# Two transformer blocks with product-key experts: six more early expert inputs, a later last sum of the gather, joint norms at the block border, and retention heads in pairs

## The chip, the cores and the metric

One core of a Trainium2 chip runs the kernel, one launch for the whole computation. The metric is the device time of one execution in microseconds (us), lower is better. PE is TensorE (PEld its weight loads), DVE is VectorE, ACT is ScalarE, POOL is GpSimd, SP is SyncE, which here issues the weight stream's DMAs.

## What is computed

256 tokens of width 1024 pass two blocks, each of depth one, all in float32. The first block modulates and normalises x, runs a bidirectional retention over 8 heads (64 key columns, 128 value columns), a Fourier mix, gates both, and adds a convolutional feed-forward of width 2816; it ends with a norm. The second block normalises again, runs an RWKV-7 and an mLSTM branch, merges them, and adds PEER: product-key retrieval among 128 x 128 single-neuron experts. Cut to what the change touches:

```python
# retention, per head; state s comes from the context tokens
intra_decay = where(diff >= 0, exp(lg * maximum(diff, 0)), 0)
o_f = (q @ k.T * intra_decay) @ v + (q * exp(lg * (pos + 1))) @ s
o = o_f + flip(o_b)                       # diagonal counts twice
# end of block 1, start of block 2
x = rms_norm(x, final_norm_w)
h = _rmsnorm(x, norm1_g)                  # norm of a norm
# PEER
s = einsum('nhpc,hpkc->nhpk', q, sub_keys)
s_top, i_top = top_k(s, 16)               # for both halves
best, pos = top_k(s_top[0][:, None] + s_top[1][None, :], 16)
expert = i_top[0] * 128 + i_top[1]        # at pos
gate = softmax(best)
act = gelu(u_emb[expert] . tok) * gate
out = sum(act * v_emb[expert])
```

## The kernel before

All activations lie transposed, features on the partitions and 256 tokens along the row. Weights come as one stream of pages of 1 MB (two blocks of 128 x 1024), which SP loads into a ring of three. Two ways of multiplying are used. In the split way ACT writes a rounded copy of a block (`split`, L1031, the "hi" part), DVE subtracts it for the rest (L1442, the "lo" part), and PE sums three fp32r products of each tile; three pairs of such pieces lie in SBUF, and `piece_used` frees them. In the `whole` way PE multiplies the fp32 block straight from the ring (L434 is the helper line of every matmul); the profile shows two MATMUL instructions for each such product.

Every engine's order is written out by hand, and semaphores carry the data flow. What the steps of the prediction touch:

**Retention** (`scores`, `outputs` on PE; `decay_exp` L1163 on ACT; `decay_arg` L1591 and the product L1612 on DVE; L360 on POOL). Head after head: DVE computes the exponent (L1593, L1594), ACT its Exp (L1165), POOL multiplies by a mask that doubles the diagonal (L360), DVE multiplies the scores by it (L1612), PE forms the output, ACT copies it (L1172). There are two buffers of each kind. Even heads use partitions 0 to 63 of the array's rows, odd heads 64 to 127. The Fourier products follow (L434 on `fT`).

**Block border** (`x_norm`). The last residual of block one, its squares on ACT (L1078), their sum by a matmul with ones, Ln and Exp on ACT (L1084, L1085), eight scalings on DVE into x (L1500); then squares, sum, Ln, Exp and eight scalings once more for block two's input h, and its hi and lo parts.

**Search** (`select`, `gather` L1991 on DVE, `number` L405 and L411 on POOL). For each of 8 heads DVE finds the 16 best keys of both halves for 256 tokens, forms the pair sums (L2017, L2019), finds the 16 best pairs, and marks their places (L1983). POOL turns the marks into key numbers: two multiplications (L405) and three halvings (L411). DVE does the last halving (L1991), for the head before, ahead of its own pair sums. Meanwhile PE makes queries and key scores, then the inputs of seven early experts (`early_up`), whose gelus ACT writes into `early`.

**Scatter.** After the transposes of the choice (L948) and an eighth early input, the gates of every token are laid out as a 128 x 128 matrix, first key by second key: a product of two one-hot matrices per token. DVE writes the column one-hots (L2086) and half of the row one-hots (L2083), ACT the other half (L1383 Square, L1390 Relu), PE multiplies, and ACT copies four tokens at a time into G (L1372). It is a loop of 16 tokens a pass; PSUM banks 6, 7, 0 and 1 take turns.

**Experts.** Expert e's input product (`up`, 24 fp32r matmuls of 256 columns) gives its activation, ACT its gelu (L1405), DVE multiplies by the gates and splits the result (`gate`, L2102, L2105, L2107), and `down` (12 matmuls of 512 columns) adds its output to four PSUM banks. First come six `down` alone, for experts whose inputs were made early; then a loop of 120 pairs of `down(e - 2)` and `up(e)`; then two `down`. The first page's split lies before the scatter: on ACT amid the early gelus, on DVE just ahead of the one-hots.

The modulation weights of the feed-forward come by 16 loads that POOL issues (L347), each after a step of DVE, two under way at most; their descriptors use a scratch area at the bottom of SBUF, above which `early` lies.

## Time and profile before

| what | us |
|---|---|
| median of 3 runs (lowest, highest) | 1901.5 (1900.65, 1904.35) |
| the profiled execution, its time | 1900.2 |
| its span, first to last instruction | 1898.4 |
| PE busy, share of the span | 1744.8, 92% |
| DVE busy | 1192.0, 63% |
| ACT busy | 826.4, 44% |
| POOL busy | 117.7, 6% |
| mean granted TensorE clock, as a share of full speed | 0.955 |

The profiled time is the span and 1.8 us around it. Busy shares are averages over stages with quite different limits, so they say little about one stage. A row of the timeline gives the start and the length of a run of like instructions, then engine, line, operation, tiles and count, and in brackets the engine's idle time before it with what ended it. Matmuls overlap, so their busy times add up to more than their spacing: start-to-start times are what counts. A granted clock of 1.00 is 2.4 GHz and 0.50 is 1.2 GHz; values between are mixtures over a stretch.

### The profile page before, as it was taken

What the parts mean: (1) busy time and instruction counts of PE and PEld (TensorE: products, weight loads), DVE (VectorE), ACT (ScalarE), POOL (GpSimd) and SP (SyncE); (2) the same over time, 40 slices, a digit from 0 to 9 for tenths busy, and PEclk for the clock granted to TensorE, in tenths of its full rate; (3) what the DMA queues carried; (4) which work ended last, traced back from release to release, by engine and by line L of the source; (5) the groups of instructions that cost most, each with busy time, mean ns of one, the idle gap of its engine ahead of it and who ended that gap; (6) DMA issues with size and microseconds to landing.
All of it is one profiled execution on the core that took longest, in us unless ns stands there. A gap on an engine that the chain in (4) does not pass through costs nothing.

```text
span 1898.4 us, 31715 instructions
## 1 busy us (share of the span) xinstructions
PE 1744.8 (92%) x11856; PEld 1584.1 (83%) x11856; DVE 1192.0 (63%) x2141; ACT 826.4 (44%) x1236; POOL 117.7 (6%) x130
## 2 busy tenths in 40 slices
PE   8799899899999979698899677999999999999997
PEld 1799868899998967596788566799999999999997
DVE  0647456577644658741448899666666666666665
ACT  2334435466544466221331299344444444444443
POOL 0000010022100000140003300000000000000000
PEclk9899899899999979796799899999999999999999
DMA  8566304455553522100234210455555555555553
GB/s 319 210 261 244 112 25 154 168 179 183 178 178 117 190 93 67 45 1 1 89 111 134 89 45 0 146 186 184 192 180 195 179 193 181 189 187 184 192 180 119
DMA packets 38521, 279.03 MB, mean 147 GB/s; under 512 B 4401, under 2 KB 4529, under 8 KB 5041
## 3 DMA queue, kind: packets, MB, share of 16 engines
q1 hardware_dynamic: 35136, 254.82, 39.3%
q0 software_dynamic: 2304, 16.78, 2.3%
q10 hardware_dynamic: 1008, 6.41, 0.9%
q8 instruction: 53, 0.87, 0.2%
q14 instruction: 20, 0.16, 0.0%
HBM read 276.94 MB, written 1.05 MB: 146 GB/s over the span
## 4 chain that ended last, share of the span: by engine, by line
PE 78%; DVE 10%; ACT 6%; POOL 2%; issue 2%; DMA 1%; ACTq 0%; SPq 0%; POOLq 0%; DVEq 0%
PE ps L434 78%; DVE piece L1442 1%; DMA ring<-in_stream 1%; ACT small L1383 1%; POOL arena L405 1%; POOL arena L411 1%; ACT piece L1031 1%; DVE arena L1752 1%; DVE arena L1983 1%; ACT small L1390 1%; DVE arena L1921 0%; DVE arena L1500 0%; DVE arena L1525 0%; DVE arena L1844 0%; ACT arena L1138 0%
## 5 line engine op out<-in xcount | busy, mean ns | idle before, releaser
L434 PEld LDWEIGHTS ps<-h_r,piece 128*128 128x128 f32 x5808 | 727.5, 195 | 38.0 <-issue 25.4
L434 PE MATMUL ps<-h_r,piece 128*128 128x256 f32 x5808 | 735.3, 287 | 22.1 <-DVE h_r L1506 9.5
L1442 DVE TENSOR_TENSOR piece<-ring,piece 128x1024 fp32r<-128x1024 f32 x440 | 541.9, 1238 | 309.3 <-ACT piece L1031 309.3
L1031 ACT ACTIVATE piece<-ring 128x1024 fp32r<-128x1024 f32 x440 | 461.6, 1056 | 401.9 <-PE ps L434 387.1
L434 PE MATMUL ps<-piece,late_r 128*128 128x512 f32 x1536 | 373.6, 393 | 6.0 <-DVE late_r L2107 6.0
L434 PEld LDWEIGHTS ps<-piece,late_r 128*128 128x128 f32 x1536 | 281.6, 189 | 60.9 <-issue 5.7
L2102 DVE TENSOR_TENSOR late<-late,arena 128x256 f32<-128x256 f32 x120 | 76.5, 637 | 125.9 <-ACT late L1405 125.9
L434 PE MATMUL ps<-arena 128*64 128x128 f32 (+8 forms) x696 | 124.3, 373 | 29.5 <-DVE hx L1855 9.0
L434 PEld LDWEIGHTS ps<-arena 128*128 128x128 f32 (+4 forms) x696 | 93.8, 203 | 57.0 <-issue 14.7
L1405 ACT ACTIVATE late<-ps 128x256 f32<-128x256 f32 x120 | 46.2, 385 | 213.4 <-PE ps L434 213.4
L434 PE MATMUL ps<-arena,ring 128*128 128x256 f32 x384 | 85.9, 384 | 1.6 <-DVE arena L1500 1.6
L434 PEld LDWEIGHTS ps<-arena,ring 128*128 128x128 f32 x384 | 73.4, 193 | 11.9 <-issue 2.0
L1053 ACT ACTIVATE arena<-ps 128x512 f32<-128x512 f32 x43 | 25.7, 597 | 107.0 <-PE ps L434 107.0
L434 PE MATMUL ps<-ffn_hi,piece 128*128 128x256 f32 x352 | 63.5, 283 | 0.8 <-DVE piece L1442 0.8
L2107 DVE TENSOR_TENSOR late_r<-late,late_r 128x256 fp32r<-128x256 f32 x128 | 54.4, 425 | 4.4
L434 PE MATMUL ps<-hx,arena 128*128 128x128 f32 (+1 forms) x352 | 50.9, 285 | 6.4 <-DVE hx L1855 5.6
L434 PEld LDWEIGHTS ps<-ffn_hi,piece 128*128 128x128 f32 x352 | 54.9, 192 | 1.0 <-DVE piece L1442 1.0
L434 PE MATMUL ps<-mg_hi,piece 128*128 128x256 f32 x256 | 49.2, 294 | 6.0 <-DVE mg_lo L1468 6.0
L434 PE MATMUL ps<-arena,pconst_sb 128*128 128x256 f32 (+1 forms) x136 | 48.7, 505 | 4.4 <-ACT arena L1078 2.6
L434 PEld LDWEIGHTS ps<-hx,arena 128*128 128x128 f32 (+1 forms) x352 | 45.1, 196 | 6.9 <-DVE hx L1855 5.9
L434 PE MATMUL ps<-ffn_lo,piece 128*128 128x256 f32 x176 | 49.8, 283 | 0.0
L434 PEld LDWEIGHTS ps<-mg_hi,piece 128*128 128x128 f32 x256 | 42.3, 203 | 6.3 <-issue 6.3
(298 smaller groups left out, 1821.2 us busy)
## 6 DMA issues: line engine op xcount, KB each, us to landing
ring<-in_stream SPq DMA_DIRECT2D x240, 1024.0 KB, 5.0
arena<-in_mod POOLq DMA_DIRECT2D x16, 1024.0 KB, 5.9
arena<-in_const ACTq DMA_DIRECT2D x1, 2256.0 KB, 8.7
arena<-in_const ACTq DMA_DIRECT2D x1, 2000.0 KB, 9.3
xres<-in_xT SPq DMA_DIRECT2D x1, 1024.0 KB, 10.3
arena<-in_xT SPq DMA_DIRECT2D x1, 1024.0 KB, 12.3
arena<-in_subk ACTq DMA_DIRECT2D x1, 1024.0 KB, 4.9
out<-arena SPq DMA_DIRECT2D x2, 512.0 KB, 2.7
```

The lines of the kernel that those rows point to most:

```text
L405: g.tensor_tensor(e[:, 2 * c:2 * c + 2], e[:, 2 * c:2 * c + 2], topf[:, :, 2 * hh + c, :].unsqueeze(2).to_broadcast([P, 2, 16, 16]), ALU.m ...
L411: g.tensor_tensor(e[:, :, :, 0:m], e[:, :, :, 0:m], e[:, :, :, m:2 * m], ALU.add).then_inc(S["place_no"], 1)
L434: mm_last[0] = nc.tensor.matmul(*args, **kw)
L1031: A(piece[:, 0, c % 3], ring[:, p % RING, s], ACT.Copy).then_inc(S["hi_ready"], 1)
L1053: A(dst, ps[:, T % 2, src], func, **kw).then_inc(acc_free[T % 2], 1)
L1383: a = A(r[:, e, :], iota, ACT.Square, scale=-1.0, bias=selT[:, 0, bass.ds(16 * i + (4 * b + e), 1)])
L1390: A(r, r, ACT.Relu, scale=-1.0, bias=1.0).then_inc(S["row_hot"], 1)
L1405: A(gelu_t[:, e % 2, :], ps[:, T % 2, 0:L], ACT.Gelu).then_inc(acc_free[T % 2], 1)
L1442: TT(piece[:, 1, c % 3], ring[:, p % RING, s], piece[:, 0, c % 3].bitcast(F32), ALU.subtract).then_inc(S["lo_ready"], 1)
L1752: ins = STT(mqk[:, n, :], mqk_raw[:, n, tap:tap + L], cols[:, cq + 5 * n + tap:cq + 5 * n + tap + 1], mqk[:, n, :], ALU.mult, ALU.add)
L2102: TT(a_t, ready, G[:, :, bass.ds(LOOP * i + e, 1)].rearrange("p n a -> p (n a)"), ALU.mult).then_inc(S["a_chain"], 1)
L2107: TT(a_r[:, 1, b, :], a_t, a_r[:, 0, b, :].bitcast(F32), ALU.subtract).then_inc(S["a_ready"], 1)
```

## The change

- `EARLY` goes from 8 to 14. Of these, `CHOICE` = 10 are made where the eight were: nine before the transposes of the choice, the tenth after them. Four are made amid the scatter: each has 8 product steps, one behind each of 8 of 14 groups of four tokens, into bank 1, and its gelu is on ACT at group 13, 27, 41 and 55. The gates use three banks instead of four. PE's and ACT's part of the scatter is written out, 64 groups; DVE's stays a loop.
- The loop has 114 experts, and 12 `down` alone stand before it.
- The first page's hi part is copied by POOL, after its key numbers; DVE's lo part follows the one-hots.
- `gather(hh - 1)` moves behind the second search of `select(hh)`.
- At the border two sums are formed from the same squares, one with ones and one with weights `norm_w` = `final_norm_w`^2 + eps; h is scaled straight from x with `gain12` = `final_norm_w` x `norm1_g_2`. The block's own norm of x comes behind the first split of the next stage.
- In the retention POOL's mask is gone: ln 2 on the diagonal is added within the exponent. Scores and outputs are formed for two heads at a time, the 64-row matmuls of both heads in turn; there are four buffers of `probs`.
- `SCRATCH` goes from 4096 to 1024, and `h_full` moves to where G is written last.

```diff
-EARLY = 8
-SCRATCH = 4096
+EARLY = 14
+CHOICE = 10
+SCRATCH = 1024
...
-        h_full = w3(0, 8)
+        h_full = w3(30720, 8)
-        probs = w3(28160, 2, 512)
+        probs = w3(0, 4, 512)
-        gate_banks = (6, 7, 0, 1)
+        gate_banks = (6, 7, 0)
...
# POOL
-            pool.wait_ge(S["const1_in"], 16)
-            for hh in range(8):
-                pool.wait_ge(S["decay_exp"], hh + 1)
-                g.tensor_tensor(decay[:, hh % 2], decay[:, hh % 2], c1("mask12"), ALU.mult).then_inc(S["decay_m"], 1)
...
             for hh in range(7):
                 number(hh)
+            first = PAGE["first"]
+            for s in range(2):
+                c = piece_no(first) + s
+                if s == 0:
+                    pool.wait_ge(loaded[first % RING], 16 * (first // RING + 1))
+                pool.wait_ge(S["piece_used"], c - 1 - s)
+                g.tensor_copy(piece[:, 0, c % 3], ring[:, first % RING, s]).then_inc(S["hi_ready"], 1)
...
# PE, retention
+            def scores(m):
+                if m:
+                    pe.wait_ge(S["probs"], 2 * m)
+                for st in range(2):
+                    for e in range(2):
+                        r = 64 * e
+                        s_ = mm(ps[:, 4 + e, st * L:(st + 1) * L], qk[r:r + 64, 4 + m, st * P:(st + 1) * P],
+                                qk[r:r + 64, m, :], start=True, stop=True)
+                        if st == 1:
+                            s_.then_inc(S["scores"], 1)
+
+            def outputs(m):
+                pe.wait_ge(S["probs"], 2 * m + 2)
+                if m:
+                    pe.wait_ge(S["o_sb"], 2 * m)
+                for e in range(2):
+                    n = 2 * m + e
+                    for st in range(2):
+                        mm(ps[:, 6 + e, 0:L], v_tok[:, st, n * P:(n + 1) * P], probs[:, n % 4, st * L:(st + 1) * L],
+                           start=st == 0, stop=False)
+                for d, st_ in enumerate((st_f, st_b)):
+                    for e in range(2):
+                        r = 64 * e
+                        o = mm(ps[:, 6 + e, 0:L], st_[r:r + 64, m * P:(m + 1) * P], qdec[r:r + 64, 4 * d + m, :], start=False,
+                               stop=d == 1)
+                        if d == 1:
+                            o.then_inc(S["out_mm"], 1)
...
+            for m in range(4):
+                if m < 3:
+                    scores(m + 1)
+                outputs(m)
...
# PE, border
-            x_norm(1)
-
-            x_norm(2)
+            for k in range(8):
+                if k % 2 == 0:
+                    pe.wait_ge(S["xs_sq"], 4 + (k // 2 + 1))
+                mm(ps[:, 2, 0:L], ones, sq[:, k, :], start=k == 0, stop=k == 7)
+                m = mm(ps[:, 3, 0:L], norm_w[:, k, :], sq[:, k, :], start=k == 0, stop=k == 7)
+            m.then_inc(S["xs_mm"], 1)
...
# PE, scatter
+            def early_step(n):
+                e, k = CHOICE + n // 8, n % 8
+                T, p = TURN["peer"] + e, PAGE["early"] + e // 2
+                if k == 0:
+                    turn(T)
+                    turn(T + 1)
+                    pe.wait_ge(loaded[p % RING], 16 * (p // RING + 1))
+                m = mm(ps[:, 1, (T % 2) * L:(T % 2 + 1) * L], ring[:, p % RING, e % 2, k, :], h_full[:, k, :], start=k == 0,
+                       stop=k == 7)
+                if k == 7:
+                    m.then_inc(S["acc_ready"], 1)
...
+            for q in range(L // 4):
+                scatter(q)
+                n, k = (q - 3) // 14, (q - 3) % 14
+                if 0 <= n < EARLY - CHOICE and k < 8:
+                    early_step(8 * n + k)
...
# ACT
-            for n in range(8):
-                act.wait_ge(S["out_mm"], n + 1)
-                A(oT[:, n, :], ps[:, 6 + n % 2, 0:L], ACT.Copy).then_inc(S["o_sb"], 1)
-                if n < 6:
-                    decay_exp(n + 2)
+            for m in range(4):
+                if m < 3:
+                    decay_exp(2 * m + 2)
+                    decay_exp(2 * m + 3)
+                for n in range(2 * m, 2 * m + 2):
+                    act.wait_ge(S["out_mm"], n + 1)
+                    A(oT[:, n, :], ps[:, 6 + n % 2, 0:L], ACT.Copy).then_inc(S["o_sb"], 1)
...
-            x_norm(1)
-
-            for u in range(4):
-                x_squares(u)
-            x_norm(2)
+            act.wait_ge(S["xs_mm"], 2)
+            ac(A(rs, ps[:, 3, 0:L], ACT.Ln, scale=1.0 / D, bias=eps_sq))
+            A(rs, rs, ACT.Exp, scale=-0.5).then_inc(S["xs_root"], 1)
             for k in range(8):
                 act.wait_ge(S["hraw"], 24 + k + 1)
                 A(h[0][:, k, :], sq[:, k, :], ACT.Copy).then_inc(S["h_hi"], 1)
+            ac(A(rs_last, ps[:, 2, 0:L], ACT.Ln, scale=1.0 / D, bias=eps6))
+            A(rs_last, rs_last, ACT.Exp, scale=-0.5).then_inc(S["xs_root"], 1)
...
-            for e in range(5):
+            for e in range(CHOICE - 2):
                 early_gelu(e)
-            split(PAGE["first"])
...
+            for q in range(L // 4):
+                if q % 2 == 1:
+                    rows(q)
+                if q >= 2 and q % 4 != 1:
+                    gates_out(q - 2)
+                if q % 2 == 1:
+                    rows_end(q)
+                if q >= 2 and q % 4 == 1:
+                    gates_out(q - 2)
+                if late_e < EARLY and q == 13 + 14 * (late_e - CHOICE):
+                    T = TURN["peer"] + late_e
+                    act.wait_ge(S["acc_ready"], T + 1)
+                    A(early[:, late_e, :], ps[:, 1, (T % 2) * L:(T % 2 + 1) * L], ACT.Gelu).then_inc(acc_free[T % 2], 1)
+                    late_e += 1
...
# DVE
-                dv(TS(d, c1("dist_f"), lgrow[:, n:n + 1], None, ALU.mult))
+                dv(STT(d, c1("dist_f"), lgrow[:, n:n + 1], c1("ln2_same"), ALU.mult, ALU.add))
                 STT(d, c1("dist_b"), lgrow[:, 8 + n:9 + n], d, ALU.mult, ALU.add).then_inc(S["decay_arg"], 1)
...
+            TT(norm_w, ones.unsqueeze(1).to_broadcast([P, 8, P]), square1.unsqueeze(2).to_broadcast([P, 8, P]), ALU.mult)
             residual("dn", 40)
-            x_norm(1, xres, col("final_norm_w", 0, 8))
+            x_norm(1, sq, gain12)
+            stage("lora", 1)
+            dve.wait_ge(S["xs_root"], 3)
+            for k in range(8):
+                STT(xres[:, k, :], xres[:, k, :], last_w[:, k:k + 1], rs_last, ALU.mult, ALU.mult).then_inc(S["xfin"], 1)
...
                 second_places(srcs, vals, idxs, ready)
-                if hh:
-                    gather(hh - 1)
                 cd, u, v = cand[:, hh % 2], topv[:, :, 2 * hh, :], topv[:, :, 2 * hh + 1, :]
...
                 found[hh] = second_places(srcs, vals, idxs, ready)
+                if hh:
+                    gather(hh - 1)
...
-            split(PAGE["first"])
...
             with dve.Fori(1, L // 16) as i:
                 onehots(i)
+            split(PAGE["first"])
             dve.wait_ge(S["g_sb"], L // 4)
```

## Rows read from the trace of the kernel before

**Rows 1.** The page, part 4: chain of waits, shares of the span by engine.
```profile
PE 78%; DVE 10%; ACT 6%; POOL 2%; issue 2%; DMA 1%; ACTq 0%; SPq 0%; POOLq 0%; DVEq 0%
```
**Rows 2.** Busy time by stage: stretch, length, PE, PEld, DVE, ACT, POOL, clock, DMA.
```profile
1072.00:1093.00 21.00, 4.33 (x16) 3.51 (x15) 19.29 (x86) 3.43 (x7) 4.85 (x5) 0.62 0.15 50
1093.00:1184.40 91.40, 68.85 (x524) 61.90 (x522) 85.17 (x286) 87.01 (x225) 0.00 (x0) 0.99 0.06 23
1184.40:1208.40 24.00, 18.71 (x72) 14.41 (x72) 16.08 (x27) 6.37 (x6) 0.00 (x0) 0.93 0.28 91
1208.40:1883.00 674.60, 674.56 (x4321) 615.66 (x4322) 447.17 (x600) 289.00 (x359) 0.00 (x0) 1.00 0.54 183
```
**Rows 3.** Timeline of PE, second products alone, then the loop's first.
```profile
1194.51 5.72 PE L434 MATMUL ps<-piece,late_r 128*128 128x512 f32 x24 [1.30 <-DVE late_r L2107]
1201.53 5.70 PE L434 MATMUL ps<-piece,late_r 128*128 128x512 f32 x24 [1.30 <-DVE late_r L2107]
1208.44 3.02 PE L434 MATMUL ps<-piece,late_r 128*128 128x512 f32 x12 [1.21 <-DVE late_r L2107]
```
**Rows 4.** Timeline from the end of the search to the scatter's start.
```profile
1066.07 0.38 ACT L1053 ACTIVATE early<-ps 128x256 f32<-128x256 f32 x1 [3.07 <-PE ps L434]
...
1089.61 1.51 PE L948 MATMUL ps<-pconst_sb,arena 128*128 128x128 f32 x6 [16.67 <-DVE arena L2074]
...
1090.92 5.13 PE L434 MATMUL ps<-arena,ring 128*128 128x256 f32 x16
...
1097.44 0.69 DVE L2083 TENSOR_TENSOR row_more<-pconst_sb,late 128x512 f32<-128x512 f32 x1 [3.01 <-PE ps L434]
```
**Rows 5.** Timeline: two early gelus, a pass of the scatter, the first gate.
```profile
1085.04 0.66 ACT L1053 ACTIVATE early<-ps 128x256 f32<-128x256 f32 x2
...
1129.81 0.63 ACT L1390 ACTIVATE late<-late 128x512 f32<-128x512 f32 x1
...
1133.62 0.71 PE L434 MATMUL ps<-pconst_sb,small 128*128 128x128 f32 x4 [1.01 <-ACT small L1390]
...
1135.06 0.61 PE L434 MATMUL ps<-cols,late 128*128 128x128 f32 x4
...
1135.24 0.63 ACT L1390 ACTIVATE late<-late 128x512 f32<-128x512 f32 x1
...
1184.39 0.60 DVE L2102 TENSOR_TENSOR late<-early,arena 128x256 f32<-128x256 f32 x1 [2.59 <-ACT arena L1372]
```
**Rows 6.** Timeline of the retention: DVE and POOL, and the first Fourier weight loads.
```profile
240.68 0.75 DVE L1594 SCALAR_TENSOR_TENSOR arena<-arena,small 128x512 f32<-128x512 f32 x1
...
242.65 0.69 DVE L1612 TENSOR_TENSOR arena<-ps,arena 128x512 f32<-128x512 f32 x1 [1.23 <-POOL arena L360]
...
249.58 1.27 POOL L360 TENSOR_TENSOR arena<-arena 128x512 f32<-128x512 f32 x1 [1.63 <-ACT arena L1165]
249.66 1.74 DVE L1594 SCALAR_TENSOR_TENSOR arena<-arena,small 128x512 f32<-128x512 f32 x1
...
262.74 1.38 PEld L434 LDWEIGHTS ps<-arena 128*128 128x128 f32 x7 [0.33 <-issue]
```
**Rows 7.** The search: DVE's waits for POOL (total, times, longest), and one head's timeline.
```profile
DVE arena L1991 <- POOL arena L411: 9.2, 7, 1.3
...
1077.50 2.52 POOL L411 TENSOR_TENSOR arena<-arena 128x512 f32<-128x512 f32 x3
...
1080.24 0.28 DVE L2017 TENSOR_TENSOR arena<-arena 128x128 f32<-128x128 f32 x1
```
**Rows 8.** Busy time of a stretch of gram products, columns as in rows 2.
```profile
774.90:778.20 3.30, 3.29 (x28) 2.84 (x28) 2.12 (x4) 0.00 (x0) 0.00 (x0) 1.00 0.43 181
```
**Rows 9.** Timeline ahead of and at the block border.
```profile
503.36 2.36 DVE L1442 TENSOR_TENSOR piece<-ring,piece 128x1024 fp32r<-128x1024 f32 x2 [2.31 <-ACT piece L1031]
...
562.34 3.62 PE L434 MATMUL ps<-arena,pconst_sb 128*128 128x256 f32 x16
...
573.85 0.47 ACT L1084 ACTIVATE small<-ps,cols 128x256 f32<-128x256 f32 x1 [1.69 <-PE ps L434]
```

More of the change, by code:

```diff
@@ L939, in _, with early_up @@
             m.then_inc(S["x_in_psum"], 1)
-            for e in range(EARLY - 1):
+            def early_up(e):
+                T = TURN["peer"] + e
+                turn(T)
+                whole(PAGE["early"] + e // 2, e % 2, ps[:, T % 2, 0:L]).then_inc(S["acc_ready"], 1)
+            for e in range(CHOICE - 1):
                 early_up(e)
@@ L1359, in _ @@
                 A(selv[:, tt, 2, :], selv[:, tt, 2, :], ACT.Exp).then_inc(S["g_exp"], 1)
-            for e in range(5, EARLY - 1):
-                early_gelu(e)
+            early_gelu(CHOICE - 2)
             act.wait_ge(S["x_in_psum"], 1)
@@ L1394, in _, with rows @@
-            act.wait_ge(S["selt_sb"], 2)
-            rows(0)
-            with act.Fori(1, L // 16) as i:
-                rows(i)
-            gates_out(L // 16 - 1, 2)
-            gates_out(L // 16 - 1, 3)
+            def rows(q):
+                r = row_hot[q % 4]
+                if q >= 4:
+                    act.wait_ge(S["g_mm"], 2 * q - 6)
+                for e in range(4):
+                    a = A(r[:, e, :], iota, ACT.Square, scale=-1.0, bias=selT[:, 0, 4 * q + e:4 * q + e + 1])
+                a.then_inc(S["row_square"], 1)
```

137 lines of the change are left out of this document (50 added, 87 removed).

## The prediction

> **What bounds the kernel now.** I read the chain of waits by engine first: 78% of it is TensorE (PE), 10% VectorE (DVE), 6% ScalarE (ACT) [rows 1]. Then busy time by stage [rows 2]. From 1208.4 to 1883.0 us runs the expert loop, 120 experts in 674.6 us, 5.62 us each, with PE busy throughout: there time goes only if PE gets less work. Three stages ahead of it are bound otherwise. While the keys are searched (1072 to 1093) DVE is busy for 19.3 of 21 us and PE for 4.3. In the scatter (1093 to 1184.4) DVE (85.2 of 91.4 us) and ACT (87.0) are full and PE has room. From 1184.4 to 1208.4, second products alone, no engine is full. So this change is priced by the wait that ends last in each stage. What the measurement can tell from no change is 0.2%, 3.8 us.
>
> **The change, part by part.** I count against the profiled execution's own 1900.2 us (span 1898.4).
>
> *Six more early inputs.* Six experts leave the loop and join the stage of second products alone. In the loop each costs 5.62 us, 33.7 together. There, a pair of second products takes from 1194.51 to 1201.53 to 1208.44, 6.97 us on average, with PE idle for 1.2 to 1.3 us before each pair [rows 3]: the next page's second copy starts only when the pair's second product has taken its piece, and behind the copy come DVE's subtraction and gates. The code of this stage is unchanged, so three more pairs cost 20.9. Gain 33.7 - 20.9 = **12.8 us**; bounds 12 to 16.8 (PE work alone, 5.7 a pair).
>
> *Where the six products go.* One costs 8 steps of 0.43 us, 3.45 us from one gelu to the next [rows 4]. Two go into the search. Before, PE was idle for 16.67 us ahead of the transposes at 1089.61 [rows 4], and 6.9 us fit in it.
>
> *Four amid the scatter.* A full pass of 16 tokens lasts from 1129.81 to 1135.24, 5.43 us, and ACT has no idle in it [rows 5]. On PE two groups of four tokens take from 1133.62 to 1135.06 + 4 x 0.11, 1.9 us with the first fill, 0.89 a group. With a step in every group PE would need 4 x (0.89 + 0.43) = 5.3 us of the 5.43: it just fits, and only 8 of 14 groups carry a step. A step delays the next group by up to 0.43 us, and DVE and ACT have about 0.5 us before they need what PE frees. So the products cost nothing on the path. If that cover is gone, they cost 32 x 0.43 = 13.8 us, which is a rival. ACT is full, so its four gelus count: 0.33 us each [rows 5], with hand-over **+1.1 us** (0 to 1.5). Three gate banks in place of four change nothing: the copy asked for is always one behind ACT's last Relu.
>
> *First page's copies on POOL.* The page is loaded after the tenth early gelu, so POOL copies it in the scatter's first 15 us. The trace shows no such copy. What it shows is POOL and DVE side by side: a DVE operation of 0.75 us took 1.74 us when it began 0.08 us after a POOL operation of 1.27 us [rows 6], so DVE stood still for POOL. POOL's 512 elements with two inputs took 1.27; twice 1024 elements with one input cost between 2 x 1.27 and 4 x 1.27, less the 1.1 us by which DVE runs ahead of PE. Bounds 0 to +4.0; I take **+1.8**, near the lower end, as one input is read instead of two. The Trainium skill, "SBUF — State Buffer", section "Who interferes with whom", says that a DVE instruction with two SBUF inputs, or in a two-port mode, and a GpSimd instruction exclude each other for their whole length. By that rule alone both copies would be paid in full, +2.5 to +5. DVE's subtraction of this page moves behind the scatter, where DVE was idle for 2.59 us before its first gate [rows 5]; two operations of 1.2 us fit. Cost 0 (to +0.3).
>
> *The last early product.* It took 5.13 us for 16 matmuls at 1090.92, not 3.45: PE had been idle, and the granted clock was 0.62 in that stretch [rows 2, 4], so part of it ran at 1.2 GHz. DVE then waited 3.01 us for PE [rows 4]. With two more products PE now works until 1.3 us before the transposes. The product runs at 2.4 GHz: **-1.6 us** (-1.7 to 0). ACT now computes the gates' Exp after the eighth gelu and pays two table switches: **+0.4** (0 to 1.5).
>
> *Gather behind the second search.* DVE waited seven times for POOL's last sum, 9.2 us together [rows 7]. The sum is wanted 2.5 us later now, when POOL is done. But the two pair sums (L2017, L2019) that follow move up into POOL's three operations, which end at 1080.02 [rows 7], and they read two SBUF inputs as L1594 does. What is late next is the lock: between nothing gained and 9.2. POOL's work is three instructions, DVE waits only for the one under way, so I take 0.4 us lost a head: **-6.5 us**.
>
> *Retention in pairs.* Before, a head took about 2.9 us and DVE waited for POOL's mask at its start and end (1.23 us at 242.65) [rows 6]. Now POOL is gone, DVE has two operations of 0.75 and one of 0.69 us a head, 2.2 with hand-over, and PE interleaves the two row groups. That these overlap is seen in the gram products: 28 matmuls of alternating groups took 3.30 us [rows 8], when 20 of 256 columns at 0.216 (3.45 / 16 of the early product) and 8 of 128 at 0.11 would make 5.2 in sequence. So PE needs 0.9 + 1.7 + 0.9 + 0.2 = 3.7 us a pair and DVE 4.5: DVE is the bound. The first pair's probabilities are ready at 242.7 as before, then five decays and six products, 12.0 us, give 254.7. PE ends later: the third pair's outputs at 255.5, their copies at 256.3, the last outputs at 259.0. Before, the Fourier products began at 262.74 [rows 6]. **-3.7 us** (-5 to +2.5; the upper end if the groups don't overlap).
>
> *Joint norms.* Before: a sum from 562.34, 16 matmuls in 3.62 us, its root, eight scalings, squares, and a second sum whose root began at 573.85 [rows 9]. Now one stretch of 32 matmuls, 7.1 us, ends at 569.4 and the root follows: **-4.4 us** (-3.5 to -4.7). The scalings of x go behind a split and push the next one by 1.4 us, against 3.4 of lead. The added weights (about 1.9 us of DVE) fit into 2.31 us of idle at 501 [rows 9].
>
> *Smaller descriptor scratch.* It concerns POOL's 16 modulation loads alone, two of them under way at most; cost 0 (to +3).
>
> Sum: -12.8 + 1.1 + 1.8 - 1.6 + 0.4 - 6.5 - 3.7 - 4.4 = -25.7, so 1874.5 for the profiled execution. The median of the runs lies 1.3 us above it: **1875.8 us**.
>
> **Rivals.**
> A. *The scatter doesn't hide the steps.* PE in order, 5.3 of 5.43 us, every wait a little longer than counted: then the steps add up to 13.8 us. For it: the margin of 0.1 us. Against: steps in 8 of 14 groups only. 1889.6.
> B. *Row groups give nothing, or DVE stalls in the retention.* PE then needs 5.5 us a pair from 242.7, ending at 265: +2.5 in place of -3.7. For: head by head the same shapes ran one after the other at 0.216. Against: rows 8. 1882.
> C. *Slower: the scatter written out starves PE.* Sixteen passes of a loop become 64 groups in a line, so each instruction is fetched anew. To eat 25.7 us it must lengthen each group from 1.36 to 1.76 us; at 1.85 the 64 groups cost 31.4 and the time is 1875.8 + 31.4 = 1907. For: nothing in the loop shows fetching. Against: the gram stretch, itself in a line, ran 28 matmuls and 28 weight loads in 3.30 us [rows 8], 17 a us, where the scatter needs some 15.
>
> **How the numbers follow.** Forecast 0.74, A 0.12, B 0.07, C 0.07. C is slower by over 0.2% with 0.04 and within it with 0.03. From the forecast's own bounds: search at its best and no lock for POOL's copies give -32 (1869.5); search at -2, copies at +4 give -19 (1882). With some room for clock windows of a few us and for B, the range is 1867 to 1886; it leaves out A and C, 0.19. Faster 0.93, same 0.03, slower 0.04.
>
> **What would show it.** The loop still at 5.62 us with 114 experts; six pairs of second products at 7.0 us; a scatter pass at 5.4 us with PE idle gone; the product ahead of the scatter near 3.5 us; no wait of L1991's successor for POOL, but a pair sum longer than 0.28 us; a retention pair at 4.5 us on DVE; one sum of 7.1 us at the border. The prediction is wrong if scatter passes with steps take over 5.8 us, or if second products alone take over 7.5 us a pair.

## The result and the profile after

The changed kernel takes **1876.9 us** (median of 4 runs, 1875.7 to 1877.8) against 1901.1 (4 runs): ratio 0.9868, 95% interval 0.9855 to 0.988. It is faster; the forecast was 1875.8. The profiled execution took 1877.8 us (span 1876.0), 22.4 less than the profiled one of before, against a sum of 25.7. The engines' chain of waits answers to [rows 1]: POOL has gone from it (2% before), ACT has 4% instead of 6%, and PE has the rest, 82% instead of 78%.

```profile
PE 82%; DVE 10%; ACT 4%; issue 2%; DMA 1%; DVEq 0%; SPq 0%; POOL 0%; ACTq 0%; POOLq 0%
```

To see where time went I cut both executions at the same ten events: start, first scores, first Fourier product, end of the block's last products, first lora product, first search, transposes of the choice, scatter's first product, first `down`, first loop product with its `down`, last `down`. Columns as in [rows 2]: stretch, length, PE, PEld, DVE, ACT, POOL, clock, DMA. First before:

```profile
0.00:237.54 237.54, 212.32 (x1481) 179.00 (x1481) 115.15 (x123) 83.48 (x113) 10.14 (x21) 0.96 0.62 229
237.54:262.74 25.20, 23.40 (x97) 15.96 (x96) 19.42 (x23) 8.88 (x18) 9.48 (x7) 1.00 0.13 42
262.74:562.22 299.48, 286.96 (x2241) 279.93 (x2241) 189.26 (x244) 159.88 (x231) 32.50 (x44) 0.98 0.48 162
562.22:578.54 16.32, 9.01 (x35) 7.06 (x34) 7.87 (x20) 10.68 (x19) 0.12 (x1) 0.90 0.18 65
578.54:998.96 420.42, 368.06 (x2674) 336.93 (x2675) 224.37 (x331) 159.11 (x229) 31.32 (x22) 0.87 0.24 81
998.96:1089.61 90.65, 73.98 (x385) 65.98 (x385) 80.00 (x482) 16.70 (x27) 34.15 (x35) 0.93 0.34 115
1089.61:1096.72 7.11, 6.43 (x22) 5.25 (x23) 4.82 (x11) 1.62 (x5) 0.00 (x0) 0.69 0.00 0
1096.72:1185.92 89.20, 65.80 (x513) 59.68 (x513) 85.19 (x283) 86.37 (x224) 0.00 (x0) 1.00 0.06 24
1185.92:1214.16 28.24, 24.44 (x108) 19.61 (x109) 18.35 (x29) 8.49 (x8) 0.00 (x0) 0.94 0.34 112
1214.16:1888.18 674.02, 674.02 (x4309) 614.69 (x4308) 444.79 (x598) 287.27 (x358) 0.00 (x0) 1.00 0.54 183
```

Then after:

```profile
0.00:241.62 241.62, 215.87 (x1481) 183.35 (x1481) 115.41 (x123) 83.49 (x113) 8.88 (x20) 0.94 0.60 225
241.62:265.55 23.93, 19.03 (x97) 13.08 (x97) 15.98 (x23) 8.50 (x17) 0.00 (x0) 0.86 0.13 45
265.55:564.07 298.52, 285.69 (x2241) 278.68 (x2240) 192.14 (x249) 160.14 (x232) 33.15 (x44) 0.98 0.46 162
564.07:575.99 11.92, 7.19 (x35) 6.04 (x34) 4.61 (x12) 6.02 (x13) 0.12 (x1) 0.89 0.25 89
575.99:997.17 421.18, 366.58 (x2674) 334.89 (x2675) 227.59 (x338) 159.90 (x231) 31.32 (x22) 0.88 0.23 81
997.17:1079.28 82.11, 80.90 (x417) 72.07 (x417) 78.66 (x481) 15.57 (x27) 35.11 (x35) 1.00 0.39 140
1079.28:1084.26 4.98, 4.30 (x23) 3.57 (x23) 2.74 (x9) 1.51 (x5) 0.00 (x0) 1.00 0.00 2
1084.26:1175.15 90.89, 77.31 (x576) 70.49 (x577) 88.57 (x285) 87.56 (x228) 2.02 (x2) 0.99 0.11 37
1175.15:1225.48 50.33, 42.64 (x180) 33.69 (x181) 33.17 (x53) 14.86 (x14) 0.00 (x0) 0.94 0.41 144
1225.48:1865.78 640.30, 640.30 (x4093) 583.91 (x4092) 423.16 (x568) 272.83 (x340) 0.00 (x0) 1.00 0.52 183
```

Line by line the differences are:

| stretch | seen | my terms for it |
|---|---|---|
| up to the first scores | +4.1 | 0 |
| retention | -1.3 | -3.7 |
| between it and the border | -1.0 | 0 |
| border | -4.4 | -4.4 |
| mixers up to the search | +0.8 | 0 |
| search up to the transposes | -8.5 | -6.5 + 0.4 |
| transposes to scatter | -2.1 | -1.6 |
| scatter | +1.7 | +1.1 + 1.8 |
| second products alone, then six experts fewer in the loop | +22.1 - 33.7 | +20.9 - 33.7 |
| sum | -22.4 | -25.7 |

The total came out nearly right because errors in both directions met: the retention brought a third of its term, the search more than its term, and 4.1 us were lost where nothing was changed. The experiments are about these three, and about whether the scatter really hides its steps.

### The profile page after: what moved, and what is told of

The parts are those of the page before. It is cut to its first block, busy times and chain, and to the rows that moved or that the text cites. A ratio compares the mean times of both kernels' runs of the same rounds, so it can differ in the third digit from the quotient of the medians.

```text
span 1876.0 us, 31040 instructions
## 1 busy us (share of the span) xinstructions
PE 1740.2 (93%) x11808; PEld 1579.8 (84%) x11808; DVE 1184.8 (63%) x2140; ACT 814.3 (43%) x1223; POOL 110.6 (6%) x124
## 4 chain that ended last, share of the span: by engine, by line
PE 82%; DVE 10%; ACT 4%; issue 2%; DMA 1%; DVEq 0%; SPq 0%; POOL 0%; ACTq 0%; POOLq 0%
PE ps L443 81%; DVE piece L1479 1%; DMA ring<-in_stream 1%; ACT piece L1062 1%; DVE arena L1793 1%; DVE pconst_sb L2126 1%; DVE cols L2126 0%; DVE late L2126 0%; DVE arena L1536 0%; DVE arena L1559 0%; DVE arena L1885 0%; ACT arena L1096 0%; DVEq L2126 0%; DVE late L2143 0%; ACT arena L1166 0%
## 5 line engine op out<-in xcount | busy, mean ns | idle before, releaser
L443 PEld LDWEIGHTS ps<-h_r,piece 128*128 128x128 f32 x5664 | 708.6, 195 | 37.0 <-issue 25.4
L443 PE MATMUL ps<-h_r,piece 128*128 128x256 f32 x5664 | 716.3, 286 | 21.6 <-DVE h_r L1540 9.5
L1479 DVE TENSOR_TENSOR piece<-ring,piece 128x1024 fp32r<-128x1024 f32 x434 | 535.0, 1239 | 307.4 <-ACT piece L1062 305.9
L1062 ACT ACTIVATE piece<-ring 128x1024 fp32r<-128x1024 f32 x432 | 453.3, 1056 | 408.9 <-PE ps L443 395.8
L443 PE MATMUL ps<-arena 64*128 64x256 f32 (+7 forms) x712 | 126.4, 386 | 34.1 <-DVE arena L1826 8.8
L2143 DVE TENSOR_TENSOR late<-late,arena 128x256 f32<-128x256 f32 x114 | 72.7, 638 | 119.6 <-ACT late L1441 119.6
L443 PEld LDWEIGHTS ps<-arena 128*128 128x128 f32 (+3 forms) x712 | 94.9, 210 | 60.6 <-issue 20.5
L443 PE MATMUL ps<-arena,ring 128*128 128x256 f32 x480 | 110.5, 379 | 1.6 <-DVE arena L1536 1.6
L443 PEld LDWEIGHTS ps<-arena,ring 128*128 128x128 f32 x480 | 88.1, 190 | 12.3 <-issue 2.0
L1084 ACT ACTIVATE arena<-ps 128x512 f32<-128x512 f32 x43 | 25.7, 597 | 107.0 <-PE ps L443 107.0
```

The source lines that it names most:

```text
L443: mm_last[0] = nc.tensor.matmul(*args, **kw)
L1062: A(piece[:, 0, c % 3], ring[:, p % RING, s], ACT.Copy).then_inc(S["hi_ready"], 1)
L1084: A(dst, ps[:, T % 2, src], func, **kw).then_inc(acc_free[T % 2], 1)
L1479: TT(piece[:, 1, c % 3], ring[:, p % RING, s], piece[:, 0, c % 3].bitcast(F32), ALU.subtract).then_inc(S["lo_ready"], 1)
L2143: TT(a_t, ready, G[:, :, bass.ds(LOOP * i + e, 1)].rearrange("p n a -> p (n a)"), ALU.mult).then_inc(S["a_chain"], 1)
```

## The experiments

Medians are of 4 or 5 runs of a kernel (11 of the one with only the scratch changed). The kernel before ran beside each of the three sets: 1900.5 us (beside the changed kernel again, PE filled, DVE's order and the gather), 1901.3 (beside the scratch, both kernels on the steps and the short copy) and 1902.8 (beside the other four). It moved by 2.3 us without any change, so a difference of up to 2.3 us across sets is read from the traces. Unless something else is named, a difference in us is against the changed kernel's 1876.6.

**The changed kernel again.** No edit.

> The changed kernel itself, run again beside the others, as their base. Its first median was 1876.9 us (1875.7 to 1877.8). If the 4.1 us that its trace had lost before the retention belong to the change (the smaller descriptor scratch or the new order of the program), a second trace shows them again at the same place, PE's first bg product near 225.8 us. If they are stretches at the lower TensorE clock that fall here or there from run to run, the second trace has them elsewhere or not at all (near 221.7 to 222.7), with nothing else moved before 225 us.

1876.6 us (1875.1 to 1878.1), ratio 0.9872 (0.9857 to 0.9887). The first scores again start at 241.4 us. So the 4.1 us aren't chance from run to run: it and each of its ten variants below have a stretch at the lower clock that begins between 133.8 and 138.2 us, and before has none. The changed kernel's row shows it by the clock column and by the matmul count, 54 where before had 78 in the same 9 us:

```profile
134.00:143.00 9.00, 9.00 (x54) 9.00 (x54) 1.23 (x1) 1.25 (x2) 0.53 (x1) 0.63 0.70 253
```

**Only the descriptor scratch.**
```diff
 # the kernel before
-SCRATCH = 4096
+SCRATCH = 1024
```

> The kernel before with the smaller descriptor scratch and nothing else. Every trace of the changed kernel and of its variants has a stretch at the lower TensorE clock at 136 us (6.8 us, costing 3.1), and before has none there; no instruction of the change runs there, but the smaller scratch does. Theory 1, the scratch (or the place of things in memory) brings the stretch: it is there in this trace too, and the time is up to 3 us more than before, 1903.5. Theory 2, it comes with something else of the program (its length, its shift of 0.3 us): the trace shows none at 136 us and the time is that of before, 1900.5 (1899 to 1902). My forecast had 0 for the scratch, with +3 as its bound.

1901.8 us (1898.5 to 1904.8), ratio 1.0004 (0.9995 to 1.0013). Nothing. The same stretch is at the full clock:

```profile
134.00:143.00 9.00, 9.00 (x78) 9.00 (x78) 1.23 (x1) 1.21 (x3) 0.53 (x1) 1.00 0.69 255
```

Theory 2 holds: the scratch costs at most 2.5 us by that interval and most likely 0, and it doesn't bring the stretch. What does stays open (below).

**PE filled ahead of the first outputs.**
```diff
             pe.wait_ge(S["qdec"], 2)
+            for _ in range(16):
+                mm(ps[:, 2, 0:L], ones, v_tok[:, 0, 0:L], start=True, stop=True)
```

> Sixteen idle-filling products of 256 columns (3.5 us at the full clock) are put between the first pair's scores and the wait for its probabilities. Theory 1, the clock: PE stood idle for 3.7 us there, the granted clock then was 0.50 from 246 to 250 us and 0.70 to 254, and this took 2.4 of the 3.7 us that the pairs were to bring. With the filling the stretch stays at the full clock and the Fourier products begin 2 to 3 us earlier: 1874.4 (1873.5 to 1875.5). Theory 2, ACT's order: the Exps of the third pair stand behind the first pair's copies, whatever the clock. Then the filling gives 0.5 us or less, 1876.5, and the wait of DVE for L1193 (1.73 us) stays.

1876.8 us (1875.5 to 1876.9). By the time alone theory 2 would stand. The trace says otherwise. In the changed kernel the first outputs' pair begins at 246.47 and the Fourier products at 265.55; here it is 249.06 and 265.41. The changed kernel's stretch, then this one's timeline row of the filling, and its stretch:

```profile
246.47:265.55 19.08, 17.89 (x88) 12.36 (x89) 11.28 (x16) 4.79 (x11) 0.00 (x0) 0.84 0.00 1
```
```profile
241.95 7.17 PE L443 MATMUL ps<-arena,pconst_sb 128*128 128x256 f32 x32
```
```profile
249.06:265.41 16.35, 15.29 (x90) 10.57 (x89) 9.79 (x14) 4.27 (x10) 0.00 (x0) 1.00 0.00 1
```

My filling was twice too long: one such product is two matmul instructions, so 16 made 32 and took 7.17 us, and everything behind began 2.6 us late (3.3 counted from the first scores, which begin at 240.89 here and at 241.62 in the changed kernel). With the clock kept at 1.00 the rest then took 16.35 instead of 19.08 us. So the lower clock does cost 2.7 us there, and the experiment paid them out again in its own filling. ACT's order isn't it: DVE's wait of 1.73 us for L1193, which the changed kernel's rows below show at 254.72, has gone without any change on ACT.

**DVE's order in the retention.**
```diff
                 TT(probs[:, n % 4, :], ps[:, 4 + n % 2, :], decay[:, n % 2, :], ALU.mult).then_inc(S["probs"], 1)
-                if n < 6:
-                    dve.wait_ge(S["probs"], n + 1)
-                    decay_arg(n + 2)
+                if n < 6 and n % 2 == 1:
+                    dve.wait_ge(S["probs"], n)
+                    decay_arg(n + 1)
+                    dve.wait_ge(S["probs"], n + 1)
+                    decay_arg(n + 2)
...
 # also: decay_arg(1) ahead of the page's split on DVE, decay_exp(1) ahead of bg_page(5) on ACT
```

> DVE takes both probabilities of a pair first and then the two decays of the next pair, and the second head's decay stands before the split of the page behind, on DVE and on ACT. Nothing is added. The first outputs start from 244.0 to 244.4 instead of 246.4 us, so PE idles for 1.3 to 1.6 us instead of 3.7. Theory 1, the clock: it is not lowered by so short an idle time, and the end of the retention comes 2.5 to 4 us earlier: 1873.5 (1872.5 to 1874.7). Theory 2, DVE's chain alone sets the end: the last pair's probabilities come only as much earlier as the first one's do, 0.8 us: 1876.1.

1871.5 us (1864.7 to 1873.8), ratio 0.9832 (0.9812 to 0.9852): 5.1 less than the changed kernel. The five runs fall into two groups, 1864.7 and 1864.8 against 1871.5, 1873.3 and 1873.8. The trace is of the run of 1873.3; where the two others won some 7 to 9 us more is open, so the 5.1 is loose and the reading rests on the trace. First the changed kernel's timeline (start, length, instruction, idle before it and who ended it), then this one's and its stretch by windows:

```profile
243.46 0.68 DVE L1646 TENSOR_TENSOR arena<-ps,arena 128x512 f32<-128x512 f32 x1
...
246.47 1.65 PE L443 MATMUL ps<-arena 64*128 64x256 f32 x6 [3.72 <-DVE arena L1646]
...
254.72 0.69 DVE L1646 TENSOR_TENSOR arena<-ps,arena 128x512 f32<-128x512 f32 x1 [1.73 <-ACT arena L1193]
```
```profile
242.12 1.29 DVE L1648 TENSOR_TENSOR arena<-ps,arena 128x512 f32<-128x512 f32 x2 [0.17 <-PE ps L443]
...
243.55 7.74 PE L443 MATMUL ps<-arena 64*128 64x256 f32 x42 [1.47 <-DVE arena L1648]
...
246.22 0.68 DVE L1648 TENSOR_TENSOR arena<-ps,arena 128x512 f32<-128x512 f32 x1
...
250.57 0.68 DVE L1648 TENSOR_TENSOR arena<-ps,arena 128x512 f32<-128x512 f32 x1
```
```profile
240.95:260.07 19.12, 16.46 (x98) 11.33 (x97) 14.64 (x21) 8.73 (x16) 0.00 (x0) 1.00 0.15 56
```

PE is idle for 1.47 us, not 3.72, and the clock stays up: 19.12 us in place of 23.93, 4.8 less. Of these 2.6 are the clock's (16.52 from the first outputs' pair to the Fourier products, against 19.08) and 2.2 the earlier start. The pair's rhythm is 4.35 us (246.22 to 250.57), DVE's own work: my 4.5.

**The retention head by head again** (PE, ACT, DVE and POOL as before, with POOL's mask).
```diff
-            for m in range(4):
-                if m < 3:
-                    scores(m + 1)
-                outputs(m)
+            for n in range(8):
+                if n < 7:
+                    scores(n + 1)
+                outputs(n)
```

> The changed kernel with the retention head by head again and POOL's mask. Theory 1, what the traces of before and after say: the pairs brought 1.3 us (39.7 against 41.0), so +1.3 and, as the head-by-head order keeps PE at the full clock, no stretch at the lower clock at 246 us: 1877.9. Theory 2, as forecast: +3.7, 1880.3. Theory 3, the pairs bring nothing in time, since what the order wins the clock takes: 0 or below, 1876.6. Second question: if the stretch at the lower clock at 136 us goes away with this part (POOL's mask, the larger place for probabilities), it comes with it.

1879.0 us (1876.9 to 1880.7), +2.4. Its stretch takes 25.20 us with the clock at 1.00, as before to the hundredth; so +1.3 are the stretch's, Theory 1, and the rest lies within what the medians can tell. The pairs brought 1.3 us, where another order of the same instructions brings 6.1 (25.20 to 19.12).

**Gather ahead of the second search again.**
```diff
                 second_places(srcs, vals, idxs, ready)
+                if hh:
+                    gather(hh - 1)
...
                 found[hh] = second_places(srcs, vals, idxs, ready)
-                if hh:
-                    gather(hh - 1)
```

> The wait for POOL's last sum stands again between the first and the second search of a head; all else as in the changed kernel. Theory 1, the whole wait was gained (9.2 us in the trace of before, and after has no wait of DVE for POOL and pair sums of 0.28 and 0.26 us): +8.5 to +9.5, 1885.9. Theory 2, as forecast, the pair sums pay 0.4 us a head to POOL: +6.5, 1883.4. Theory 3, the period of a head is shorter for another reason (PE's key scores no longer in the way, fewer instructions): +4 or less, 1880.9 or below.

1884.5 us (1884.0 to 1887.5), ratio 0.9915 (0.9901 to 0.9928): +7.9; the profiled execution is the slowest of the five. Its search takes 90.70 us, where the changed kernel has 82.11: +8.6, with the old wait. And the last product ahead of the scatter is slow again (DVE's waits: total, times, longest; then PE's timeline):

```profile
DVE arena L2032 <- POOL arena L412: 9.2, 7, 1.3
```
```profile
1087.03 1.51 PE L966 MATMUL ps<-pconst_sb,arena 128*128 128x128 f32 x6 [9.80 <-DVE arena L2115]
1088.33 5.08 PE L443 MATMUL ps<-arena,ring 128*128 128x256 f32 x16
```

Theory 1. In the changed kernel the same three are: no wait, 1.22 us of idle ahead of L966 at 1079.28, and 3.62 us for the product. The forecast's 0.4 us a head for the pair sums wasn't there, since it is POOL that waits: DVE's sum took 0.27 us beside POOL in all seven heads (0.28 before), while POOL's second of three operations went from 0.72 to 0.86 us. The timeline of one head, and the three operations' shortest, median and longest time in ns, before and after:

```profile
1066.39 2.67 POOL L412 TENSOR_TENSOR arena<-arena 128x512 f32<-128x512 f32 x3
...
1067.57 0.27 DVE L2056 TENSOR_TENSOR arena<-arena 128x128 f32<-128x128 f32 x1
```
```profile
L411 POOL TENSOR_TENSOR arena<-arena x21: 397/719/1265, 1011.2 to 1079.6; 128x512 f32<-128x512 f32 x7, 128x256 f32<-128x256 f32 x7, 128x128 f32<-128x128 f32 x7
```
```profile
L412 POOL TENSOR_TENSOR arena<-arena x21: 397/856/1266, 1009.4 to 1068.7; 128x512 f32<-128x512 f32 x7, 128x256 f32<-128x256 f32 x7, 128x128 f32<-128x128 f32 x7
```

The full clock of the last product, which I had put down to the two more products, needs the gather's place too: with the ten products kept and the gather back, PE is idle for 9.80 us and the product takes 5.08. So of the 10.7 us between first search and scatter the gather's move brought 8.6 directly and 2.1 through the clock, which the two products alone don't. The changed kernel's wait of 2.1 us for the gates' Exp isn't in this trace: it shows only once the gather is out of the way, and the 8.6 are net of it.

**The norms one behind the other again** (the border's PE, ACT and DVE part as before).
```diff
-                mm(ps[:, 2, 0:L], ones, sq[:, k, :], start=k == 0, stop=k == 7)
-                m = mm(ps[:, 3, 0:L], norm_w[:, k, :], sq[:, k, :], start=k == 0, stop=k == 7)
-            m.then_inc(S["xs_mm"], 1)
+            x_norm(1)
+            x_norm(2)
```

> The changed kernel with the two norms at the block border one behind the other again, as before. Theory 1, as forecast: +4.4, 1881.0 (the stretch from the sum to the first lora product 4.4 us longer, 16.2 instead of 11.8). Theory 2, the shorter stretch was given back later (the x scalings behind the lora split delay the next pages): +2 or less, 1878.6. Second question: if the stretch at the lower clock at 136 us goes away with this part, the part's place in the program brings it.

1880.3 us (1878.6 to 1880.6), +3.8, of which up to 2.3 can be the set's. The trace decides: the border takes 16.32 us again, +4.40. Of it 0.7 come back later, up to the search (420.5 us against 421.2), and 0.3 ahead of it, where PE's idle time behind the added weights, 1.15 us at 506.49 in the changed kernel, is 0.84 again, as before. Theory 1, less these 1.0 us.

**The scatter without its steps.**
```diff
+                if k < 7:
+                    return
```

> Of the eight steps of each of the four products amid the scatter only the last is left, with the same waits and gelus (28 steps of 0.43 us, 12.0 us of PE work, are left out, and what those four experts put in is not their full product). Theory 1, as forecast: PE has the room, the scatter takes the 85 to 86 us that it takes with the steps, and the time stays at 1876.6 (1875.3 to 1877.5). Theory 2, the steps are paid (the changed kernel's scatter did end 1.6 us late against before): up to 12 us less on the path, 1864.6; if they are paid in part, as much as the scatter is shorter. What would be left for the gelus and POOL's copies in theory 1 is 1.6 us.

1875.3 us (1874.7 to 1877.0), -1.3 between medians. The scatter takes as long as with the steps, while PE is busy for 8.4 us less:

```profile
1082.31:1173.12 90.81, 68.92 (x521) 62.04 (x521) 88.54 (x285) 87.55 (x228) 2.15 (x2) 0.99 0.11 37
```

90.81 against 90.89: the steps cost 0.1 us. Theory 1.

**Each step twice.**
```diff
+                for again in range(2):
+                    m = mm(ps[:, 1, (T % 2) * L:(T % 2 + 1) * L], ring[:, p % RING, e % 2, k, :], h_full[:, k, :],
+                           start=k + again == 0, stop=k == 7 and again == 1)
```

> Each of the 32 steps amid the scatter is done twice (13.8 us more of PE work; the products come out doubled). In a stretch of eight groups with steps PE then needs 8 x (0.89 + 0.86) = 14.0 us, where DVE and ACT take 8 x 1.33 = 10.7. Theory 1, the stretch just fits, as forecast: PE becomes the bound there and each product costs up to 3.3 us, less 0.5 to 1 of slack: +9 to +13, 1887.5. Theory 2, PE has far more room than I counted, since the steps' 0.43 and the groups' 0.89 overlap with the fill of the next: +4 or less.

1886.3 us (1884.7 to 1887.7), +9.8. The scatter takes 100.73 us, 9.84 more, 2.5 a product. So in the stretches with steps one step a group fits and a second one doesn't: of 13.8 us more PE work 4.0 were hidden. Rival A fell for the change as made; the limit that it feared lies one step further, and there it costs 9.8 us, not the whole 13.8.

**A short copy on POOL.**
```diff
-                g.tensor_copy(piece[:, 0, c % 3], ring[:, first % RING, s]).then_inc(S["hi_ready"], 1)
+                g.tensor_copy(piece[:, 0, c % 3, 0, 0:8], ring[:, first % RING, s, 0, 0:8]).then_inc(S["hi_ready"], 1)
```

> POOL copies 8 of 1024 elements of each half of the first page, so its two operations are short (the first page's high parts are then not those of its weights). In the changed kernel's trace one DVE operation beside each of POOL's two copies took 1.12 and 1.06 us instead of 0.34. Theory 1, DVE stands still while POOL copies, and DVE is close to the bound: those two take 0.34 again and the scatter ends 0.8 to 1.6 us earlier: 1875.4. Theory 2, it is hidden, as ACT is the bound and has other room: 0, 1876.6. Theory 3, as forecast by its size, 1.8 us: 1874.8.

1874.1 us (1873.4 to 1875.8), -2.5. Its scatter takes 90.28 us, 0.6 less; 1.3 more come from the stage behind, where the stretch at the lower clock was 3.4 instead of 6.8 us long (0.97 against 0.94), which I can't put down to the copy. Of its -4.4 against the changed kernel's profiled execution 2.0 lie ahead of the first scores, where nothing was changed. In the changed kernel's timeline two DVE operations, 0.60 us together elsewhere, take 2.11 beside the copies:

```profile
1088.84 2.11 DVE L2126 TENSOR_SCALAR cols<-pconst_sb,late 128x128 f32<-128x128 f32 x2
1088.85 2.02 POOL L424 CAST piece<-ring 128x1024 fp32r<-128x1024 f32 x2 [19.78 <-DMA ring<-in_stream]
```

DVE loses 1.5 us, and 0.6 of them reach the scatter's end: each of its two operations lasts about as long as the copy of 1.04 us beside it. The Trainium skill, "SBUF — State Buffer", section "Who interferes with whom", has one engine wait for the other's whole instruction where DVE's uses the ports that both share; this trace agrees in the main, with 1.5 us lost beside 2.02. The pair sums above hardly test that rule, since little of them lies beside one and the same POOL operation: in each of the seven heads the first sum begins only 0.08 to 0.09 us before POOL's first operation ends, and about 0.27 us of the two sums are left when its second begins, which is the one that lost 0.14 us.

**Gates between the halves.** Behind the scatter DVE subtracted both halves of a page and then took the gates of both experts. The changed kernel's PE rows are those of [rows 3] over again, now six times:

```profile
1184.81 5.72 PE L443 MATMUL ps<-piece,late_r 128*128 128x512 f32 x24 [1.27 <-DVE late_r L2148]
1191.83 5.73 PE L443 MATMUL ps<-piece,late_r 128*128 128x512 f32 x24 [1.30 <-DVE late_r L2148]
```
```diff
-                split(PAGE["first"] + e // 2)
+                split(PAGE["first"] + e // 2, halves=(0,))
                 early_gate(e)
+                split(PAGE["first"] + e // 2, halves=(1,))
                 early_gate(e + 1)
```

> In the stage of second products alone DVE takes the gates of an expert between the subtractions of the two halves of a page, not behind both. Nothing is added. My reading of that stage: a pair's first product waits for a chain of 1.05 (ACT's copy), 1.2 (DVE's subtraction) and 1.4 us (the gates), which begins when the product ahead of it begins and takes 2.8. With the gates ahead of the subtraction the chain is 1.4 or 1.05, then 1.2, and is over in time. Theory 1: a pair takes 5.6 to 5.7 us instead of 7.0, six pairs, -7.5 to -8: 1868.9 (1868 to 1870). Theory 2, the wait is for ACT's copy (or for the page itself), and the gates are late anyway: 0 to -2, 1875.6.

1866.3 us (1865.3 to 1867.7), ratio 0.9809 (0.9796 to 0.9823): 10.2 less than the changed kernel. PE has no idle time left in the stage, and it takes 41.06 in place of 50.33 us, 9.3 less:

```profile
1173.42:1214.48 41.06, 41.06 (x180) 34.17 (x181) 33.41 (x53) 14.87 (x14) 0.00 (x0) 0.93 0.50 177
```

Theory 1, and more than it said: the six gaps are 7.7 us of it. The rest is PE's busy time, 42.64 before and 41.06 now: without a gap ahead of it a pair takes 5.44 us, not 5.72, since its first matmuls overlap the last ones of the pair ahead. So a pair behind the first went from 7.02 to 5.44 us.

**Three reorderings together** (the two above, and on ACT the Exp ahead of the eighth gelu).
```diff
-            for e in range(CHOICE - 2):
+            for e in range(CHOICE - 3):
                 early_gelu(e)
...
+            early_gelu(CHOICE - 3)
             early_gelu(CHOICE - 2)
```

> Three reorderings together, nothing added or left out: the retention's order of ret_args (measured: -4.8 in the trace, -5.1 between medians), the gates between the halves of gate_between, and the Exp of the expert gates ahead of the eighth gelu on ACT, for which DVE waited 2.1 us in the search (PE ends its ninth product 1.2 us before the transposes, so -1.2, with the two table switches as many as before). If the three lie one behind another on the path, their gains add: 1876.6 - 4.8 - 7.7 - 1.2 = 1862.9 (1861.5 to 1864.5). If the last of them is eaten by PE's next product, 1864; if the lower clock of the stretches around eats the gain of one, 1866 to 1868.

**1861.2 us** (1861.0 to 1862.3), ratio 0.9784 (0.977 to 0.9797). Its three edits only reorder, and it is faster than both kernels: 15.4 us below the changed kernel, 41.6 below the one before. By its trace: retention 19.12 us, search 80.73 (1.4 less, the Exp's part), second products alone 39.94. Stretch by stretch the three gains are all there, 4.8, 1.4 and 10.4 us; 1.1 of the 10.4 is a stretch at the lower clock of 3.4 us where the others have 6.8.

```profile
992.16:1072.89 80.73, 80.73 (x418) 72.19 (x417) 78.58 (x481) 15.20 (x26) 35.10 (x35) 1.00 0.39 135
```

PE is now busy through all of the search.

## Why the prediction was right, and where it wasn't

**Experts out of the loop: right.** The loop stays at 640.30 / 114 = 5.62 us an expert, and a pair of second products at 7.02. The stage came out at +22.1, not +20.9, so the gain was 11.6, just under my bound of 12; the 1.2 are a longer stretch at the lower clock at its start (6.8 us against 3.4; with 3.4, in the kernel with the short copy, the stage takes 49.04 us, 20.8 more than before). What I took as given was the flaw: "the code of this stage is unchanged, so three more pairs cost 20.9". I had named its chain (copy, subtraction, gates) and given 16.8 us as the bound by PE's work, but not asked whether the order could be had otherwise. It could. PE's work alone is 5.44 us a pair, less than the 5.7 that I took, so three more pairs cost 16.3 us, and the three pairs that were there already gain as well: with the new order the stage is 12.8 us longer than before (41.06 against 28.24), not 22.1.

**Four products amid the scatter: right**, with its margin: 0.1 us for the steps, and 9.8 when they are doubled. The rest of the scatter's +1.7 is 0.6 for POOL's copies, forecast at 1.8, and 1.0 for the four gelus, forecast at 1.1. ACT's Relus (L1416, L1390 before) show both. Each stands for two groups, and in both kernels they come 2.30 and 3.13 us after one another in turn, 5.44 us for a pass, with steps and without. In the changed kernel five intervals are longer: one by 0.61 us at the copies (to 1093.89), and four by 0.26, each behind a gelu. Here is an undisturbed interval of 3.13 us, then one with a gelu (L1432), of 3.39:

```profile
1096.19 0.63 ACT L1416 ACTIVATE late<-late 128x512 f32<-128x512 f32 x1
...
1099.32 0.63 ACT L1416 ACTIVATE small<-small 128x512 f32<-128x512 f32 x1
...
1101.63 0.63 ACT L1416 ACTIVATE late<-late 128x512 f32<-128x512 f32 x1
...
1102.64 0.38 ACT L1432 ACTIVATE early<-ps 128x256 f32<-128x256 f32 x1
...
1105.02 0.64 ACT L1416 ACTIVATE small<-small 128x512 f32<-128x512 f32 x1
```

So Rival C fell: the written-out scatter has the loop's rhythm. Of the copies' term the price was wrong: POOL took 2.02 us for both, less than my lower bound of 2 x 1.27, and only 0.6 of DVE's 1.5 us reached the path.

**Gather: right in kind, too small by 2.** The step that failed is "I take 0.4 us lost a head". I had it from L1594 [rows 6], an operation of 0.75 us which lay whole beside a POOL operation of 1.27. The pair sums of 0.27 lie across the border of two POOL operations and lose nothing; POOL does, off the path. That they fall there is luck of the timing: no run shows them in the midst of a long POOL operation.

**Last early product: right size, wrong reason.** It is at the full clock (-2.1 us where I had -1.6), but the two more products that I named don't bring this by themselves; it needs the gather's move, which takes PE's idle time away.

**Exp behind the eighth gelu.** DVE waited 2.1 us for it, and in the kernel with three reorderings, where it comes earlier, the search is 1.4 us shorter, against my 0.4: within the bounds of 0 to 1.5.

**Retention: the term of -3.7 that failed.** DVE is the bound at 4.35 us a pair, and the row groups overlap: the first pair's eight scores took 1.14 us, where eight at 0.216 one behind another are 1.7.

```profile
241.62 1.14 PE L443 MATMUL ps<-arena 64*128 64x256 f32 x8
```

Rival B fell. The first pair's probabilities came where I had them (246.32, less the 4.1 us lost ahead of it, is 242.2 against 242.7), and DVE's sum of decays and products was right. What I left out is PE in the meantime: it stood idle for 3.7 us, which my own numbers held, and came back at the lower clock. The first pair's outputs were then late, behind them ACT's copies, and behind these the Exp for which DVE waited 1.73 us. 2.6 us went that way: the measured -1.3 is -3.9 with 2.6 given back. The cure was on DVE, in the decay of 1.5 us that it put between two products which PE wants together.

**Border: exact at its place.** 4.40 us, and 1.0 of them given back: 0.7 behind it, and 0.3 ahead of it, where I had the added weights fit into idle time. They end in time, but POOL's operation beside them runs into DVE's next subtraction, which takes 2.68 us instead of 2.36.

**Where nothing was changed.** Of the +4.1 up to the retention 3.0 come in the stretch at the lower clock near 136 us and 0.8 in one near 198 us that is twice as long as before; 0.3 are there ahead of both. The -1.0 is a stretch at 295 us that before has and the changed kernel doesn't (-1.4), with the added weights' +0.3 against it. In the +0.8, 0.7 are the border's. My range had "some room for clock windows of a few us", and needed it. That the total of 22.4 lies within 3.3 of my 25.7 owes something to luck: the search gave 2.4 us more than its terms and the retention 2.4 less.

## What to carry to other kernels

When work is moved into a stage, ask first whether the stage's own order is good: a chain of copy, subtraction and gates that cost 1.3 us a pair was made twice as frequent by this change (three pairs became six), and putting one gate between two subtractions gave 9.3 us. Where PE waits for a pair or a group of results, produce all that it waits for before anything that serves the next group; the wait itself costs once, and the clock that falls in it costs again. And price a move together with the idle time that it takes from PE: a product's clock depended here on a gather on another engine.

## What the runs showed of the hardware

- In 3.7 us without a matmul (242.75 to 246.47) the granted clock fell to the lower level, 1.2 GHz, and stayed there for 6.8 us, 245.6 to 252.4; around 1.47 us in the reordered kernel it stayed at 2.4 GHz.
- Every version with fourteen early inputs has a stretch at the lower clock, 3.4 or 6.8 us long, which begins between 133.8 and 138.2 us after the start. Neither kernel with eight has one, although PE's matmuls are the same up to there and it has no gap from 130 us on in either. In all of them PE does 32 products of a single column just there (below: the changed kernel, then before), and the stretch begins 2.1 to 5.1 us after the first of these. A second group of 32 of this shape starts at 207.8 us before and at 211.9 after, and both kernels have a stretch at the lower clock behind its start, from 209.9 and from 214.9 us. So a fall stands behind the start of such a group in three of these four places, and why not in the fourth, at 133 us before, no run shows. It isn't the scratch, the gather, the norms, the retention or the scatter's steps, each of which was undone by itself. It costs up to 3 us and its cause stays open; the change of the first page, the early inputs' place and the written-out scatter were not tried one by one.
```profile
133.40 4.11 PE L443 MATMUL ps<-pconst_sb,arena 128*128 128x1 f32 x32
```
```profile
133.10 3.63 PE L434 MATMUL ps<-pconst_sb,arena 128*128 128x1 f32 x32
```
- Beside a POOL copy of 1.04 us DVE operations of 0.34 us took 1.12 and 1.06; DVE sums of 0.27 us that began 0.09 us before the end of one POOL sum of two inputs and ran into the next kept their length, and the second POOL sum took 0.86 us instead of 0.72.
